# Wider first products in the four SwiGLU networks of a float32 transformer kernel

## What is computed

```
for layer in (0, 1):
    x = x + 0.5 * swiglu_ffn(x, ffn1_norm, ffn1_w_in, ffn1_w_out)
    x = x + mixer(x)          # layer 0: retention and dilated attention; layer 1: stick-breaking attention
    x = x + 0.5 * swiglu_ffn(x, ffn2_norm, ffn2_w_in, ffn2_w_out)
return rms_norm(x)

def swiglu_ffn(x, g, w_in, w_out):
    h = x * rsqrt(mean(x * x) + eps) * g
    gate, up = split(h @ w_in, 2)          # 2816 columns each
    return (silu(gate) * up) @ w_out
```

## Time and profile before

| | |
|---|---|
| median of three runs | 2185.46 us (2184.45 to 2187.73) |
| the profiled execution, its own time | 2187.13 us |
| span of its instructions | 2185.3 us |
| mean granted TensorE clock | 0.999 of 2.4 GHz |
| TensorE busy | 99% of the span |
| VectorE, ScalarE, POOL busy | 70%, 55%, 14% |

### The profile page before, as it was taken

One profiled execution on the slowest core, in us unless ns is written; L12 is line 12 of the kernel. 1 busy time (PEld: TensorE's weight loads), 2 busy tenths in 40 slices (PEclk: granted clock), 3 DMA queues, 4 the chain that ended last, 5 costly groups with the idle time before them and its releaser, 6 DMA issues.

```text
span 2185.3 us, 42508 instructions
## 1 busy us (share of the span) xinstructions
PE 2164.1 (99%) x17084; PEld 2061.6 (94%) x17084; DVE 1519.5 (70%) x2635; ACT 1194.3 (55%) x2060; POOL 296.3 (14%) x273
## 2 busy tenths in 40 slices
PE   8999999999999999999999999999999999999999
PEld 8899989999999999999999999999999998989998
DVE  6767686887578677779856666676666666886664
ACT  5655465665446554566655544455445444665453
POOL 1000112000100011210002210002210220232211
PEclk9999999999999999999999999999999999999999
DMA  7335436356744354455565655345555555435554
GB/s 259 116 126 143 135 109 197 116 175 176 218 117 126 115 152 137 131 173 164 184 201 193 194 186 180 127 134 179 188 184 177 194 187 185 154 117 172 185 184 135
DMA packets 97381, 356.56 MB, mean 163 GB/s; under 512 B 10929, under 2 KB 11057, under 8 KB 97057
## 3 DMA queue, kind: packets, MB, share of 16 engines
q1 hardware_dynamic: 94752, 342.47, 49.6%
q0 software_dynamic: 2000, 10.38, 1.8%
q10 hardware_dynamic: 432, 0.99, 0.1%
HBM read 352.68 MB, written 1.12 MB: 162 GB/s over the span
## 4 chain that ended last, share of the span: by engine, by line
PE 92%; DVE 5%; ACT 2%; issue 1%; DMA 1%; DVEq 0%; ACTq 0%; SPq 0%
PE pd L1389 24%; PE pd L1400 23%; PE pd L1397 23%; PE pd L1382 6%; PE pd L1385 3%; DVE wlo L2315 2%; PE pt L1558 1%; PE ps L1389 1%; PE pd L1574 1%; PE ps L1397 1%; PE ps L1400 1%; PE ps L1533 1%; PE ps L1767 1%; PE pd L1680 1%; ACT whi L1871 1%
## 5 line engine op out<-in xcount | busy, mean ns | idle before, releaser
L1871 ACT ACTIVATE whi<-raw 128x1024 fp32r<-128x1024 f32 x618 | 651.1, 1055 | 592.4 <-PE pd L1400 498.5
L1389 PE MATMUL pd<-x,whi 128*128 128x256 f32 (+2 forms) x3328 | 973.1, 292 | 1.6 <-DVE tb L2840 1.1
L2315 DVE TENSOR_TENSOR wlo<-raw,whi 128x1024 fp32r<-128x1024 f32 x618 | 767.6, 1243 | 256.6 <-ACT whi L1871 255.6
L1400 PE MATMUL pd<-x,wlo 128*128 128x256 f32 (+2 forms) x3319 | 941.9, 284 | 0.5 <-DVE wlo L2315 0.4
L1397 PE MATMUL pd<-x,whi 128*128 128x256 f32 (+2 forms) x3319 | 941.3, 284 | 0.0
L1389 PEld LDWEIGHTS pd<-x,whi 128*128 128x128 f32 x3328 | 627.8, 189 | 27.1 <-issue 21.0
L1400 PEld LDWEIGHTS pd<-x,wlo 128*128 128x128 f32 x3319 | 626.4, 189 | 0.9 <-DVE wlo L2315 0.9
L1397 PEld LDWEIGHTS pd<-x,whi 128*128 128x128 f32 x3319 | 624.7, 188 | 2.4
L1382 PE MATMUL pd<-a,whi 128*128 128x512 f32 x528 | 184.9, 395 | 0.0
L3103 POOL TENSOR_TENSOR acc<-acc,sq 128x256 f32<-128x256 f32 (+2 forms) x78 | 74.0, 949 | 808.9 <-ACT sq L1930 807.4
L3113 POOL TENSOR_TENSOR tb<-tb,rs 128x256 f32<-128x256 f32 x88 | 122.0, 1386 | 375.3 <-ACT tb L2173 375.3
(11 more groups left out here) (391 smaller groups left out, 3322.8 us busy)
## 6 DMA issues: line engine op xcount, KB each, us to landing
raw<-in_w SPq DMA_DIRECT2D x648, 512.0 KB, 3.6
TA<-scr POOLq DMA_DIRECT2D x2, 1392.0 KB, 11.5
C<-in_c POOLq DMA_DIRECT2D x1, 2432.0 KB, 10.7
TD<-scr POOLq DMA_DIRECT2D x2, 1056.0 KB, 8.3
TD<-scr POOLq DMA_DIRECT2D x2, 768.0 KB, 13.2
h<-in_h SPq DMA_DIRECT2D x4, 272.0 KB, 5.7
out<-result SPq DMA_DIRECT2D x4, 256.0 KB, 2.5
C<-in_c POOLq DMA_DIRECT2D x1, 800.0 KB, 14.6
```

What stands on the lines that cost most here:

```text
L1389: e.matmul(out, hi, xh, start=begin, stop=False)
L1400: self.block_done(e.matmul(out, lo, xh, start=False, stop=end), c, j)
L1871: e.activation(m.whi[i][:, 0:n], m.raw[c % NRAW][:, 0:n], ACT.Copy).then_inc(*self.up("ac_hi", ("hi", c)))
L2315: e.tensor_tensor(m.wlo[i][:, 0:n], m.raw[c % NRAW][:, 0:n], m.whi[i][:, 0:n].bitcast(F32), ALU.subtract).then_inc(*self.up("dv_lo", ("lo" ...
```

## The change

In every SwiGLU stage the first tiles stay as they are: three (six in stage 4) and then NARROW_UP = 6 more. The other first tiles, 35 (32 in stage 4), become wide and read the scaled x. Scaled x is kept in the buffers yh, yl of the mixers' output, which become one tensor `y2`. scaled_x is planned from root_at + 0.2 in steps of 0.5 chunks, one k each. For a wide gate, a copy on ACT (gate_low) takes the second half of the bank and an addition on VectorE (silu_in) adds the first half; for a wide up tile, a reduction on VectorE (up_add) sums both halves and POOL multiplies the two (up_mul). Both up_add and up_mul are in the old file too, where no first tile is wide.

```
+NARROW_UP = 6
-    def scaled_x(self, stage, r0):
+    def scaled_x(self, stage, r0, every=0.1):
         for k in range(8):
-            self.step("dv", r0 + 0.05 + 0.1 * k, "z_norm", stage, k)
-            self.step(*(("ac", r0 + 0.1 + 0.1 * k) if k else ("dv", r0 + 0.04)), "z_hi", stage, k)
-            self.step("dv", r0 + 0.17 + 0.1 * k, "z_lo", stage, k)
+            r = r0 + every * k
+            self.step("dv", r + 0.05, "z_norm", stage, k)
+            self.step(*(("ac", r + 0.1) if k or stage > 3 else ("dv", r + 0.04)), "z_hi", stage, k)
+            self.step("dv", r + 0.17, "z_lo", stage, k)
...
-        self.await_root(self.dense(order[:n], True, 3))
+        first = order[:n]
+        for t in order[n + NARROW_UP:]:
+            t.x, t.wide = "w", True
+        self.await_root(self.dense(first, True, 3))
+        r0 = self.root_at
...
-            self.step("dv", g.end + 0.1, "silu_in", stage, g, j)
-            self.step("ac", g.end + 0.3, "silu", stage, j)
+            if g.wide:
+                self.step("ac", g.end + 0.1, "gate_low", stage, j, g)
+            self.step("dv", g.end + (0.3 if g.wide else 0.1), "silu_in", stage, g, j)
+            self.step("ac", g.end + (0.5 if g.wide else 0.3), "silu", stage, j)
...
+        self.scaled_x(stage, r0 + 0.2, 0.5)
...
+def y_unused(plan, stage):
+    return [("used", plan.final[stage - 1, kind]) for kind in ("y", "w") if (stage - 1, kind) in plan.final]
+
+def scaled_place(m, plan, stage, k):
+    if stage > 3:
+        return m.yh, m.yl, y_unused(plan, stage)
+    return m.xh, m.xl, [("early", stage, k)]
...
-            part = m.a2 if tile.x == "a" else m.x2
+            part = m.a2 if tile.x == "a" else m.y2
...
+    def gate_low(self, stage, j, t):
+        e, key = self.e, (stage, j, 0)
+        for s in self.ahead(("dense", t.key), self.free("tb", key)):
+            e.wait_ge(*s)
+        e.activation(self.buf("tb", key)[:, 0:T2], self.buf("pd", t.key)[:, T2:2 * T2], ACT.Copy).then_inc(
+            *self.up("ac_gate", ("gate_low", stage, j)))
...
         if t.wide:
-            for s in self.ahead(("dense", t.key), *room):
+            for s in self.ahead(("dense", t.key), ("gate_low", stage, j)):
                 e.wait_ge(*s)
-            self.both(dst, t).then_inc(*self.up("dv_out", *done))
+            e.tensor_tensor(dst, dst, self.buf("pd", t.key)[:, 0:T2], ALU.add).then_inc(*self.up("dv_out", *done))
             return
```

More of the change, by code:

```diff
@@ L1105, in __init__ @@
             self.ring[n] = [sb(f"{n}{i}", [128, 384]) for i in range(RINGS[n])]
-        self.yh, self.yl = sb("yh", [128, 8, T2], F32R), sb("yl", [128, 8, T2], F32R)
+        self.y2 = sb("y2", [128, 2, 8, T2], F32R)
+        self.yh, self.yl = self.y2[:, 0], self.y2[:, 1]
         self.ring["su"] = [sb(f"su{i}", [128, 16]) for i in range(4)]
@@ L1310, in x_unused @@
 def x_unused(plan, stage):
-    return [] if stage == 0 else [("used", plan.final[stage - 1, "x"]), ("used", plan.final.get((stage - 1, "z"), 0))]
+    return [] if stage == 0 else [("used", plan.final[stage - 1, "z" if STAGES[stage - 1][0] == "conv_ffn" else "x"])]
+def y_unused(plan, stage):
[4 more added lines that the diff above has]
+    return m.xh, m.xl, [("early", stage, k)]
 def conv_place(engine, stage, t):
@@ L1357, in moving @@
             return m.xh[:, k, at], m.xl[:, k, at], ("x_hi", stage, k), ("x_lo", stage, k)
-        if tile.x == "z":
-            return m.xh[:, k, at], m.xl[:, k, at], ("z_hi", stage, k), ("z_lo", stage, k)
+        if tile.x in ("z", "w"):
+            xh, xl, _ = scaled_place(m, self.p, stage, k)
+            return xh[:, k, at], xl[:, k, at], ("z_hi", stage, k), ("z_lo", stage, k)
         if tile.x == "m":
@@ L1838, in run @@
             "c_pe_out": self.c_pe_out, "conv_mid": self.conv_mid, "gelu": self.gelu, "act_hi": self.act_hi,
-            "silu": self.silu, "rope_out": self.rope_out, "hv_turned": self.hv_turned, "rg_tanh": self.rg_tanh,
+            "silu": self.silu, "gate_low": self.gate_low, "rope_out": self.rope_out, "hv_turned": self.hv_turned, "rg_tanh": self.rg_tanh,
             "dil_exp": self.dil_exp, "dil_turned": self.dil_turned, "y_hi": self.y_hi,
@@ L1920, in z_hi @@
         e, m, (_, at) = self.e, self.m, entering(stage)
-        for s in self.ahead(("z", stage, k), ("early", stage, k)):
+        xh, _, room = scaled_place(m, self.p, stage, k)
+        for s in self.ahead(("z", stage, k), *room):
             e.wait_ge(*s)
-        e.activation(m.xh[:, k, at], m.u8[:, k, at], ACT.Copy).then_inc(*self.up("ac_norm", ("z_hi", stage, k)))
+        e.activation(xh[:, k, at], m.u8[:, k, at], ACT.Copy).then_inc(*self.up("ac_norm", ("z_hi", stage, k)))
     def squares(self, name, stage, k, src, at, ready):
@@ L2228, in y_hi @@
         src, ready = mixed_place(m, stage, k)
-        for s in self.ahead(*ready):
+        for s in self.ahead(*ready, *y_unused(self.p, stage)):
             e.wait_ge(*s)
@@ L2346, in z_lo @@
         e, m, (_, at) = self.e, self.m, entering(stage)
-        for s in self.ahead(("z", stage, k), ("z_hi", stage, k)):
+        xh, xl, room = scaled_place(m, self.p, stage, k)
+        for s in self.ahead(("z", stage, k), ("z_hi", stage, k), *room):
             e.wait_ge(*s)
-        e.tensor_tensor(m.xl[:, k, at], m.u8[:, k, at], m.xh[:, k, at].bitcast(F32), ALU.subtract).then_inc(
+        e.tensor_tensor(xl[:, k, at], m.u8[:, k, at], xh[:, k, at].bitcast(F32), ALU.subtract).then_inc(
             *self.up("dv_norm", ("z_lo", stage, k)))
@@ L3005, in y_lo @@
         src, _ = mixed_place(m, stage, k)
-        for s in self.ahead(("y_hi", stage, k)):
+        for s in self.ahead(("y_hi", stage, k), *y_unused(self.p, stage)):
             e.wait_ge(*s)
```

## The result

| | kernel before | changed kernel |
|---|---|---|
| median | 2185.97 us (four runs) | 2208.12 us (four runs, 2207.43 to 2208.61) |
| ratio | | 1.0099, interval 1.0085 to 1.0113 |
| the profiled execution, its span | 2187.13, 2185.3 us | 2207.69, 2205.9 us |
| mean granted TensorE clock | 0.999 | 0.997 |

The account below looks back on a forecast made before the run. The prediction took TensorE's issue rate to bound the kernel. Matmul savings of 5.6 us and stalls of 19.8 us gave +14.2 us, a median of 2199.7 us, with a range of 2190 to 2208.

Parts of the forecast that it names:

- Direction and size: Whole kernel: slower by 14.2 us, 0.65%, to a median of 2199.7 us; slower was given 0.83.
- The stalls: +19.8: Starts of stages 4, 6, 7 and 9: TensorE waits for low weights, +19.8 us in all.
- the second predicted wait, at c0+6: Stage 6, chunk c0+6: low weights done at 1512.04, needed at 1510.9, so TensorE waits 1.2 us.
- z_lo stands right behind its own z_norm ... VectorE idles: VectorE's list at stage starts: it idles during the trip to ACT and back, 0.54 us of 1.3 per k.
- silu_up0 is next on VectorE, but ACT's table load stands behind z_hi2: Stage 6 start: VectorE's silu_up0 waits for the 1.28 us load, Silu and POOL; lo(c0+5) done at 1507.99.
- -5.6: Wide first products, stages 4, 6, 7, 9: 1096 blocks each 0.0051 us cheaper, 5.6 us of matmul time saved.
- The clock, a rival at 0.15: Standstills of 2.8 us halve TensorE's clock, costing up to 1.7 us in each of four stages: 2206.5; chance 0.15.
- The steady part at nothing: Beside wide tile pairs: VectorE's 4.0 us and ACT's 3.4 fit under TensorE's 5.6, so no cost.

Follow-up runs that it names:

- fill_wait: Changed kernel plus ten unused 512-column matmuls on TensorE just before chunk c0+5 in stages 6 and 9; 2208.02 us, ratio 1.0099 to the kernel before.
- narrow_z: Changed kernel with scaled x still computed but no first tile wide, so nothing reads it; 2211.16 us, ratio 1.0113 to the kernel before.
- wide_only: Changed kernel with wide first products reading unscaled x2, without z_norm, z_hi and z_lo, part of the network not computed; 2179.52 us, ratio 0.9967.
- lo_later: Changed kernel with each z_lo planned 0.5 chunks later, behind the next z_norm on VectorE; 2196.21 us, ratio 1.0038 to the kernel before.
- start_later: Changed kernel with its z steps begun 1.55 chunks later, each z_lo still right behind its z_norm; 2199.77 us, ratio 1.0064 to the kernel before.
- pad_rows: Changed kernel with y2 rows of 1088 bytes instead of 1024, nothing else; 2204.82 us, ratio 1.0084 to the kernel before.
- gap_halves: Changed kernel with 512 bytes between the high and low half of y2, rows still 1024 bytes; one run, 2207.01 us.
- both_later_pad: Changed kernel with z steps begun 1.55 chunks later, z_lo behind the next z_norm, and y2 rows of 1088 bytes; 2185.75 us, ratio 0.9998.

## Why the prediction was right, and where it was off

- **Direction and size: right.** +14.2 us was forecast, +22.2 came; 2208.12 is 0.1 us above the range's upper end (the measured ratio on the 2185.46 of the forecast gives 2207.1, inside it). The view that decided it was VectorE's list at a stage's start, not its share of the span.
- **"The stalls: +19.8": right.** 20.0 from start to start, by stage 4.8, 4.8, 5.3 and 5.1 where 5.5 (stage 6), 5.5 (stage 9), 4.7 (7) and 4.1 (4) were worked out. The sum is better than its parts: the errors in stages 6 and 9 and those in 7 and 4 cancel. In stages 6 and 9 the second predicted wait, at c0+6, did not come, because TensorE was slowed by the clock just then: in fill_wait, with the clock up, it came with 1.11 us where 1.2 were forecast. narrow_z and wide_only show the z steps as the only source of the waits.
- **"z_lo stands right behind its own z_norm ... VectorE idles": right.** 0.55 us each where 0.54 was used; lo_later priced it: 12 us of the 22, by medians.
- **"silu_up0 is next on VectorE, but ACT's table load stands behind z_hi2": right.** Forecast walk: lo(c0+5) 10.08 us after z_norm0. Measured: 1510.52 - 1500.13 = 10.39. start_later alone gave 8 us back. The two causes overlap, so their prices are not to be added.
- **"-5.6": mis-sized.** It came to 1096 x (0.3550 - 0.3533) = -1.9. The step that failed is taking the wide pace from products that read a2: the same instruction on y2, with rows of 1024 bytes, takes 0.0034 us more a block. pad_rows (0.3500) and gap_halves (0.3533) show that the row distance makes this difference; why a layout has more than one pace (0.3467 or 0.3533, 0.3500 or 0.3517) stays open.
- **The clock, a rival at 0.15: it came in two of the four stages**, +3.0 us by the profile (1.5 each where the forecast had up to 1.7) behind waits of 3.0 us, and not behind the changed kernel's waits of 2.1 us and less. It should have been a term of the sum, with part of it given back: fill_wait, without it in stages 6 and 9, was no faster. The Trainium skill (TensorE: Matmul & The Clock Gate, Why this matters for your kernels) warns of idle gaps between bursts of matmuls. The trace agrees: granted clock 0.50 behind the wait of 2.97 us.
- **The steady part at nothing: right.** up_add takes 0.69 us, the value interpolated; wide_only has all of it and waits as little as the kernel before.

20.0 + 1.0 (the matmul behind each wait) + 3.0 - 1.9 = 22.1, of the 22.2 measured.

## What to carry to other kernels

A producer that hands its result to another engine and stands next in line for the answer costs its list the whole trip each time; put the next independent item between, and keep waiting items from standing ahead of a table load. Price such a step at the busiest stretch of the list on which it lands: a share of 70% hid a stretch with no room at all. Even with every stall mended the version here only draws level (2185.75 against 2186.11), since the short waits that eight more z_norm, z_hi and z_lo a stage leave behind (4.1 us in both_later_pad) eat what 512 columns win (4.6).

## What was not expected of the hardware

- A matmul of 512 columns in two halves plus one of 256 took 0.3500 us with operand rows 1088 bytes apart, and alternately 0.346 and 0.361 (mean 0.3533) with rows 1024 apart; 512 bytes between the halves changed nothing. Yet some whole stages ran at another pace of the same layout: 2 of 28 with rows of 1024 bytes at 0.3467, 4 of 16 with 1088 at 0.3517.
- TensorE's clock fell to 1.2 GHz at waits of 3.0 us, and in lo_later at waits of 1.8 us; at waits of 2.1 us in stage 7 it fell in fill_wait, narrow_z, pad_rows and gap_halves and not in the changed kernel. Ten matmuls inside the wait kept it up. It fell as early as 1.0 us before the end of the wait (narrow_z, stage 6) and as late as 1.5 us behind it (pad_rows, stage 6). The stretch in stage 0 is absent from the profiled executions of start_later and both_later_pad, which have the same instructions there. What decides between these is open.
- POOL and VectorE lengthened each other's operations on SBUF: 0.42 to 0.97 and 0.74 to 1.1 us.
